# The triangular inverse of a gated delta rule, with the whole triangle as weights, masks applied on the way out of PSUM, and transposes for one of its products

## The reference

```python
def _gated_delta_rule(q, k, v, beta, g):
    ...
    decay = jnp.where(causal, jnp.exp(jnp.where(causal, diff, 0.0)), 0.0)
    kb = kc * bc[..., None]
    a_kk = jnp.einsum('nbhid,nbhjd->nbhij', kb, kc) * decay
    lhs = jnp.eye(CHUNK, dtype=jnp.float32) + jnp.tril(a_kk, -1)
    rhs = jnp.concatenate([vc * bc[..., None], kb * jnp.exp(G)[..., None]], axis=-1)
    sol = lax.linalg.triangular_solve(lhs, rhs, left_side=True, lower=True, unit_diagonal=True)
    u, w = sol[..., :dv], sol[..., dv:]
    ...
```

## Time and profile before

| | |
|---|---|
| median of 3 runs | 2108.77 us (2107.01 to 2109.0) |
| profiled execution, its own time | 2111.13 us |
| its span in the trace | 2109.1 us |
| TensorE busy, weight loads busy | 1738.8 us (82%), 1076.9 us (51%) |
| VectorE, ScalarE, GpSimd busy | 1359.3, 925.2, 905.4 us |
| granted TensorE clock, mean | 0.963 of full speed |
| gathers of the first mixture of experts | 174 to 815 us of the span |
| inverse stage (level 0 and the loop) | 987 to 1095 us |
| gathers of the second | 1441 to 2079 us |

### The profile page before, as it was taken

One profiled execution on the slowest core, in us unless ns is written; L12 is line 12 of the kernel. 1 busy time (PEld: TensorE's weight loads), 2 busy tenths in 40 slices (PEclk: granted clock), 3 DMA queues, 4 the chain that ended last, 5 costly groups with the idle time before them and its releaser, 6 DMA issues.

```text
span 2109.1 us, 22912 instructions
## 1 busy us (share of the span) xinstructions
PE 1738.8 (82%) x7686; PEld 1076.9 (51%) x7686; DVE 1359.3 (64%) x2924; ACT 925.2 (44%) x2363; POOL 905.4 (43%) x806
## 2 busy tenths in 40 slices
PE   8987988877787887897899977887988878778786
PEld 7985444322222222786898877785444323222222
DVE  3668667667766654698345377548677667767654
ACT  5555454444444444443234233455454444444443
POOL 3335333333333332566446288545333334333331
PEclk9998999999999999999999989998999999999999
DMA  6458999999999997342114412357999999999996
GB/s 224 135 165 315 420 420 420 421 421 421 422 422 421 421 421 311 109 132 80 41 31 117 133 61 80 119 181 301 420 421 422 421 421 421 422 421 421 422 421 283
DMA packets 102054, 637.16 MB, mean 302 GB/s; under 512 B 11264, under 2 KB 12544, under 8 KB 36272
## 3 DMA queue, kind: packets, MB, share of 16 engines
q0 software_dynamic: 75216, 543.27, 62.0%
q1 hardware_dynamic: 26720, 92.43, 14.0%
HBM read 634.61 MB, written 1.05 MB: 301 GB/s over the span
## 4 chain that ended last, share of the span: by engine, by line
PE 36%; DMA 35%; DVE 14%; ACT 7%; POOL 4%; issue 3%; SPq 0%; DVEq 0%; ACTq 0%; POOLq 0%
DMA arena<-in_uv,arena 27%; PE pb L587 15%; DMA spare<-in_uv,arena 8%; PE pb L336 4%; PE pb L338 4%; PE pb L337 4%; DVE arena L1559 3%; ACT arena L1007 3%; POOL parts L1995 2%; POOL arena L2053 1%; PE pb L409 1%; PE pb L700 1%; PE pb L714 1%; PE pb L709 1%; ACT arena L1002 1%
## 5 line engine op out<-in xcount | busy, mean ns | idle before, releaser
L587 PE MATMUL pb<-arena 128*128 128x512 f32 x1848 | 915.6, 625 | 228.0 <-ACT arena L1007 226.8
L1559 DVE SCALAR_TENSOR_TENSOR arena<-arena,pb 128x1024 f32<-128x1024 f32 x462 | 563.6, 1220 | 380.9 <-DMA arena<-in_uv,arena 380.5
L2017 POOL DMA_INDIRECT arena<-in_uv,arena x462 | 440.4, 953 | 723.7 <-PE pb L587 697.6
L587 PEld LDWEIGHTS pb<-arena 128*128 128x128 f32 x1848 | 324.6, 193 | 786.7 <-ACT arena L1007 520.0
L1995 POOL TENSOR_TENSOR parts<-ring,parts 128x512 fp32r<-128x512 f32 x228 | 337.0, 1493 | 332.8 <-ACT parts L850 311.6
L999 ACT ACTIVATE arena<-arena 128x1 f32<-128x1 f32 x512 | 103.3, 202 | 621.5 <-DVE arena L1559 562.2
L850 ACT ACTIVATE parts<-ring 128x512 fp32r<-128x512 f32 x328 | 201.9, 628 | 265.8 <-PE pb L338 260.7
L336 PE MATMUL pb<-xl,parts 128*128 128x256 f32 x704 | 223.5, 317 | 10.2 <-DVE xl L1253 6.0
L1007 ACT ACTIVATE arena<-cst,arena 128x128 f32<-128x128 f32 x512 | 205.5, 401 | 47.2 <-ACT arena L1002 0.4
L336 PE MATMUL pb<-parts,xh 128*128 128x256 f32 x608 | 183.0, 301 | 41.1 <-POOL parts L1995 30.5
L337 PE MATMUL pb<-xh,parts 128*128 128x256 f32 x704 | 202.8, 288 | 0.0
(11 more groups left out here) (289 smaller groups left out, 1872.8 us busy)
## 6 DMA issues: line engine op xcount, KB each, us to landing
ring<-in_w_in SPq DMA_DIRECT2D x108, 512.0 KB, 3.6
ring<-in_wq SPq DMA_DIRECT2D x32, 512.0 KB, 4.6
ring<-in_w_out SPq DMA_DIRECT2D x16, 512.0 KB, 3.6
arena<-in_uv,arena POOLq DMA_INDIRECT x462, 20.2
ring<-in_wa SPq DMA_DIRECT2D x8, 512.0 KB, 3.6
ring<-in_wb SPq DMA_DIRECT2D x8, 512.0 KB, 3.6
arena<-in_sk POOLq DMA_DIRECT2D x2, 1024.0 KB, 6.3
arena<-in_tail POOLq DMA_DIRECT2D x1, 1280.0 KB, 9.6
```

The source lines that it names most:

```text
L587: ins = pe.matmul(ys[hf][:, :], diags[:, k % 4, :], lands[k % LANDS][:, D + hf * 512:D + (hf + 1) * 512], start=k % (8 * K) == 0, stop=k % ...
L1559: ve.scalar_tensor_tensor(z, z, 1.0, xg[t], ALU.mult, ALU.mult, accum_out=hidden[:, k:k + 1]).then_inc(*up("v_dot", ("dot", e, k)))
L2017: gp.indirect_dma_start(lands[k % LANDS], None, rows_uv, bass.IndirectOffsetOnAxis(ap=eidx[:, k:k + 1], axis=0)).then_inc(*up(f"dma_rows{k ...
```

## The change

The weights of Y become the whole triangle `LT`, with ones set on its diagonal by a copy under a mask (VectorE, `copy_predicated`, once for each group at level 0). What Y keeps of the product is chosen on the way out of PSUM, by VectorE with one of 7 new constants `signs` (identity minus mask). The cutting of `ET` on GpSimd goes away, and `ET` with it. XT of the next level is then Y^T XT in its odd half of the columns alone (64 of 128 columns of each matrix), which VectorE copies over the old ones; X is got by transposing XT, and ScalarE copies its even half of the columns. The product dX and both subtractions are gone. TensorE's order in a step n is Y(n), XT(n-1), transposes for X(n-2). At level 0, XT is `LT` times `signs[0]`, and X its transpose, copied by ScalarE; this copy stands ahead of the Exp at L1107 in ScalarE's program. The 7 new constants make `cst` 896 columns wider.

```diff
+    for lev in range(NLEV):
+        mask = parts[4 + lev]
+        parts.append(np.eye(P) - (mask.T if lev else mask))
...
+        cst = sb("cst", 4 * P + 2 * NLEV * P)
         cols = sb("cols", 64 + 96 + 32)
...
+        signs = [cst[:, (4 + NLEV + k) * P:(5 + NLEV + k) * P] for k in range(NLEV)]
...
+            def inverse_turned(lev, g):
+                o = bank(("X", lev, g))
+                pq.wait_ge(*on(("XT", lev, g)))
+                for s in range(4):
+                    ins = pe.transpose(o[:, s * P:(s + 1) * P], XT[:, g, s, :], ident)
+                ins.then_inc(*full(("X", lev, g)))
...
-                o = bank(("E0", g))
-                pq.wait_ge(*on(("E", 0, g)))
-                for s in range(4):
-                    ins = pe.transpose(o[:, s * P:(s + 1) * P], ET[:, g, s, :], ident)
-                ins.then_inc(*full(("E0", g)))
+                inverse_turned(0, g)
...
             def inverse_y(lev, g):
                 o = bank(("Y", lev, g))
-                pq.wait_ge(*on(("E", lev, g)))
-                pq.wait_ge(*on(("X", lev - 1, g)))
+                pq.wait_ge(*on(("M", g)))
+                pq.wait_ge(*on(("taken", ("X", lev - 1, g))))
                 for s in range(4):
-                    ins = pe.matmul(o[:, s * P:(s + 1) * P], ET[:, g, s, :], X[:, g, s, :], start=True, stop=True)
+                    ins = pe.matmul(o[:, s * P:(s + 1) * P], LT[:, g, s, :], X[:, g, s, :], start=True, stop=True)
                 ins.then_inc(*full(("Y", lev, g)))
 
-            def inverse_x(lev, g):
+            def inverse_xt(lev, g):
+                o = bank(("XT", lev, g))
                 pq.wait_ge(*on(("taken", ("Y", lev, g))))
-                if lev < NLEV - 1:
-                    o = bank(("dX", lev, g))
-                    pq.wait_ge(*on(("XT", lev - 1, g)))
-                    for s in range(4):
-                        ins = pe.matmul(o[:, s * P:(s + 1) * P], XT[:, g, s, :], Y[:, g, s, :], start=True, stop=True)
-                    ins.then_inc(*full(("dX", lev, g)))
-                o = bank(("dXT", lev, g))
-                pq.wait_ge(*on(("XT", lev - 1, g)))
+                m = 2 ** lev
                 for s in range(4):
-                    ins = pe.matmul(o[:, s * P:(s + 1) * P], Y[:, g, s, :], XT[:, g, s, :], start=True, stop=True)
-                ins.then_inc(*full(("dXT", lev, g)))
-
-            before = None
-            for lev in range(1, NLEV):
-                for g in range(4):
-                    if (4 * lev + g) % 8 == 7:
-                        item()
-                    inverse_y(lev, g)
-                    if before:
-                        inverse_x(*before)
-                    before = (lev, g)
-            inverse_x(*before)
+                    z = XT[:, g, s, :].rearrange("p (n two m) -> p n two m", two=2, m=m)[:, :, 1, :]
+                    ins = pe.matmul(o[:, s * 64:(s + 1) * 64], Y[:, g, s, :], z, start=True, stop=True)
+                ins.then_inc(*full(("XT", lev, g)))
+
+            steps = [(lev, g) for lev in range(1, NLEV) for g in range(4)]
+            for n, (lev, g) in enumerate(steps):
+                if (4 * lev + g) % 8 == 7:
+                    item()
+                inverse_y(lev, g)
+                if n >= 1:
+                    inverse_xt(*steps[n - 1])
+                if n >= 2 and steps[n - 2][0] < NLEV - 1:
+                    inverse_turned(*steps[n - 2])
+            inverse_xt(*steps[-1])
...
                 copy(CT[:, 2 * c2:2 * c2 + 2, :], half(("back", c2)), ("back", c2))
+            for g in range(4):
+                copy(X[:, g], bank4(("X", 0, g)), ("X", 0, g))
             aq.wait_ge(*on("lb_less"))
             ac.activation(p2, p2, ACT.Exp).then_inc(*up("a_lb", "lb_exps"))
...
-            for lev in range(1, NLEV):
-                for g in range(4):
-                    if (4 * lev + g) % 8 == 7:
-                        item()
-                    key = ("Y", lev, g)
-                    if lev > 1:
-                        aq.wait_ge(*on(("XT", lev - 1, g)))
-                    copy(Y[:, g], bank4(key), key)
+            steps = [(lev, g) for lev in range(1, NLEV) for g in range(4)]
+            for n, (lev, g) in enumerate(steps):
+                if (4 * lev + g) % 8 == 7:
+                    item()
+                if n >= 2 and steps[n - 2][0] < NLEV - 1:
+                    lev, g = steps[n - 2]
+                    key = ("X", lev, g)
+                    copy(even(X[:, g], 2 ** lev), even(bank4(key), 2 ** lev), key)
             for g in range(4):
-                if g == 0:
-                    for z in range(4):
-                        aq.wait_ge(*on(("E", NLEV - 1, z)))
                 copy(U[:, g], bank4(("U", g)), ("U", g))
...
                 vq.wait_ge(*on(("taken", ("L", g))))
-                ve.tensor_tensor(ET[:, g], LT[:, g], bm(masks[0], 4), ALU.mult).then_inc(*up("v_inverse", ("E", 0, g)))
-                vq.wait_ge(*on(("E", 0, g)))
-                ve.tensor_tensor(XT[:, g], bm(ident, 4), ET[:, g], ALU.subtract).then_inc(*up("v_inverse", ("XT", 0, g)))
-                vq.wait_ge(*full(("E0", g)))
-                ve.tensor_tensor(X[:, g], bm(ident, 4), bank4(("E0", g)), ALU.subtract).then_inc(*taken(("E0", g)))
-                at[("X", 0, g)] = on(("taken", ("E0", g)))
+                ve.copy_predicated(LT[:, g], bm(ident.bitcast(U32), 4), bm(ones, 4)).then_inc(*up("v_inverse", ("M", g)))
+                vq.wait_ge(*on(("M", g)))
+                ve.tensor_tensor(XT[:, g], LT[:, g], bm(signs[0], 4), ALU.mult).then_inc(*up("v_inverse", ("XT", 0, g)))
...
-            def inverse_x(lev, g):
-                if lev < NLEV - 1:
-                    key = ("dX", lev, g)
-                    vq.wait_ge(*full(key))
-                    ve.tensor_tensor(X[:, g], X[:, g], bank4(key), ALU.subtract).then_inc(*taken(key))
-                    at[("X", lev, g)] = on(("taken", key))
-                key = ("dXT", lev, g)
+            def inverse_y(lev, g):
+                key = ("Y", lev, g)
                 vq.wait_ge(*full(key))
-                vq.wait_ge(*on(("XT", lev - 1, g)))
-                ve.tensor_tensor(XT[:, g], XT[:, g], bank4(key), ALU.subtract).then_inc(*taken(key))
+                ve.tensor_tensor(Y[:, g], bank4(key), bm(signs[lev], 4), ALU.mult).then_inc(*taken(key))
+
+            def inverse_xt(lev, g):
+                key, m = ("XT", lev, g), 2 ** lev
+                vq.wait_ge(*full(key))
+                ve.tensor_copy(odd(XT[:, g], m), pb[place[key]][:, 0:256].rearrange("p (s n m) -> p s n m", s=4, m=m)).then_inc(
+                    *taken(key))
                 at[("XT", lev, g)] = on(("taken", key))
 
-            before = None
-            for lev in range(1, NLEV):
-                for g in range(4):
-                    if (4 * lev + g) % 8 == 7:
-                        item()
-                    if before:
-                        inverse_x(*before)
-                    flush()
-                    before = (lev, g)
-            inverse_x(*before)
+            steps = [(lev, g) for lev in range(1, NLEV) for g in range(4)]
+            for n, (lev, g) in enumerate(steps):
+                if (4 * lev + g) % 8 == 7:
+                    item()
+                inverse_y(lev, g)
+                if n >= 1:
+                    inverse_xt(*steps[n - 1])
+                flush()
+            inverse_xt(*steps[-1])
...
-            for lev in range(1, NLEV):
-                for g in range(4):
-                    if (4 * lev + g) % 8 == 7:
-                        item()
-                    key = (("E0", g) if lev == 1 else ("Y", lev - 1, g))
-                    gq.wait_ge(*on(("full", key)))
-                    gq.wait_ge(*on(("XT", 0, g)))
-                    gp.tensor_tensor(ET[:, g], LT[:, g], bm(masks[lev], 4), ALU.mult).then_inc(*up("g_inverse", ("E", lev, g)))
+            for _ in range(3):
+                item()
```

More of the change, by code:

```diff
@@ L48 @@
     matmul = transpose = activation = tensor_copy = tensor_tensor = tensor_scalar = op
-    scalar_tensor_tensor = tensor_tensor_scan = tensor_reduce = reciprocal = memset = op
+    scalar_tensor_tensor = tensor_tensor_scan = tensor_reduce = reciprocal = memset = copy_predicated = op
     max = max_index = match_replace = dma_start = indirect_dma_start = then_inc = op
@@ L89, in build @@
         spare = sb("spare", 2 * D)
-        cst = sb("cst", 4 * P + NLEV * P)
+        cst = sb("cst", 4 * P + 2 * NLEV * P)
         cols = sb("cols", 64 + 96 + 32)
@@ L204, in build, with odd, even @@
         btv, kdv, eGv = v2(sv["beta"]), v2(sv["kd"]), v2(sv["eG"])
-        LT, X, XT, ET, Y = (region(o, 2048, g=4).rearrange("p g (s n) -> p g s n", s=4)
-                            for o in (6144, 8192, 24576, 26624, 28672))
+        LT, X, XT, Y = (region(o, 2048, g=4).rearrange("p g (s n) -> p g s n", s=4)
+                        for o in (6144, 8192, 24576, 28672))
+        def odd(ap, m):
```

(3 more changed lines are left out.)

## The result

The changed kernel takes 2094.63 us in the median of four runs (2093.54 to 2096.64); the kernel before, 2108.89 in four (2107.01 to 2109.93). The ratio is 0.9942, interval 0.9928 to 0.9956: 14.3 us less, faster by 0.6%, where 17.5 had been forecast (2091.3, range 2080 to 2100). The two profiled executions differ by 17.5 us (2111.13 and 2093.62), of which 14.0 lie in the stretch that the change touches. It took 111.5 us before and 97.5 after.

What follows compares the result with a forecast made beforehand. It took TensorE's fixed order of work in the inverse stage, 1003 to 1095 us, as the bound. Terms -9.1 - 10.0 - 3.6 + 2.9 + 2.2 + 0.1 = -17.5 us, from 2108.8, gave 2091.3; range 2080 to 2100.

Steps and rivals of the forecast that it cites:

- GpSimd leaves the loop: Inverse loop: TensorE's three waits for GpSimd's masks go, -10.0 us, and the slow clock behind them, -3.6 us.
- Nothing late next: After a weight product in the inverse loop: no new TensorE wait replaces the masks, by 0.2 us of slack.
- Transposes: Inverse loop, levels 1 to 5: 20 dX sets become groups of four transposes, 0.893 to 0.437 us each, -9.1 us.
- Half width: Inverse loop: 24 sets streaming 64 columns instead of 128 stay at 0.893 us, no gain; bounds nothing and 10.7 us.
- The row of 16 columns: Trace row of a 16-column product: instructions 0.12 us apart, the full sets' pace, taken as evidence that half width gains nothing.
- Level 0: Each group's ring (L, Q, mask, transposes, next L) lengthens by c + 0.04, c being copy_predicated's 0.69: +2.9 us over four.
- Scalar's queue: After level 0: table load and Exp behind the last X copy delay Vector and XT(1,0), +2.2 us once.
- The start: Kernel start: the constants' load grows by 448 KB; taken as costing nothing, with 1.1 us as upper end.
- rival 2: Longer waits bring the slower clock to level 0 and the four sets after: +8.4 us, 2099.7, chance 0.12.
- the narrow range: Whole kernel: the forecast case's own range, 2089 to 2096 us, from c, the start and a microsecond for run spread.

## Why the prediction was right or wrong

The range held the time, and the direction was right. By its steps:

- *GpSimd leaves the loop, -10.0 and -3.6.* Right: the waits and the slow clock behind the weight products are gone, and the run that moves only GpSimd's block shows that this term alone is 12 us of the stage, 13.8 with the wait of 1.6 that this run has in its place.
- *Nothing late next.* Right; VectorE even has `finish` done in 0.42 + 0.74 us, since GpSimd no longer runs beside it.
- *Transposes, -9.1.* Right: sets of 0.893 became 0.44, 9.0 us; 10.1 with products in their place.
- *Half width, 0.* Nearly: 0.84 for 0.893, 1.2 us more than reckoned, of bounds 0 and 10.7. The row of 16 columns was the right guide.
- *Level 0, +2.9.* Right: the ring of a group is 4.59 us (991.50 to 996.09 for L's evacuation), 0.76 more, c = 0.716: 3.0.
- *Scalar's queue, +2.2.* Right: 4.49 us from the last transposes' start to XT(1,0), 2.23 without the wait and at full clock, so 2.3. In this execution the Y sets ran at 1.2 GHz and TensorE stood still for only 0.9 of it. The table load starts 0.02 us behind the copy's end and is followed by the Exp at once; the drain that the Trainium skill counts (ScalarE: Activation LUTs, What ACT_TABLE_LOAD costs) shows nowhere, and the measurement decides.
- *The start, 0.* No run isolates it. In the profile after, the first user of the constants (L502) starts at 27.83 us, 28.64 before, and waits for nothing.

The step that failed is what the sum left out: "the clock stays at 1.00 through level 0" was taken from the kernel before and kept as the likeliest case, though the change itself lengthened the waits that it rests on. It was rival 2, with 8.4 us and a chance of 0.12; it came, from the fourth group on, in each of the five executions profiled with the waits of level 0 as they are in the change (two of the changed kernel, those with the Exp first, with full width and with products for the transposes), and in the changed kernel it costs 4.8 us. With it and the half width the sum is -17.5 + 4.8 - 1.2 = -13.9, for 14.0 in the stage. So apart from GpSimd's queue the change comes out even: -9.0 - 1.2 on TensorE against +3.0 + 2.2 + 4.8 at level 0 and behind it, which is why the run that moves GpSimd's blocks alone is as fast in the total. Forecast and the second rival were taken as alternatives where the second was a term: it should have stood in the sum, at the 1.7 to 1.9 us that a drop had cost behind single waits, or more. How long the clock stays down is not the same each time: until the first weight product in three of the five executions, until XT(1,0) in the other two.

Some of the hit is luck. The range of 2080 to 2100 had its upper end at the second rival, so it held the missing term by design; that the time also lies in the narrow range of 2089 to 2096, which left this term out, is chance. So is that the two profiled executions differ by just the forecast 17.5 us.

Of the 3.5 us between 14.0 in the stage and 17.5 in the two profiled executions' times, 1.7 lie ahead of the stage (its start at 985.7 for 987.4), in unchanged code, and 1.7 behind it. The changed kernel's own two profiled executions start the stage at 985.7 and 983.2, so such differences are the spread of executions; medians differ by 14.3. The prediction had called time gained outside 987 to 1100 us a sign of being wrong, which a single pair of executions can't show.

## What to carry to other kernels

Look first at what stands in front of the late instruction in its own engine's queue: here moving three blocks of GpSimd's program, each behind four small masks, was worth as much as rewriting the algorithm. When a change takes work off TensorE or lengthens its waits, cost the granted clock as a term of the sum; if waits can't be shortened, give TensorE other work in them. The cheapest gains were in the order of the work: a group ahead, and a product that fills the waits.

## What the runs showed of the hardware that was not expected

- Behind three waits of 2.2 us with TensorE about half busy (6.91 of 13.43 us) the granted clock fell to its lower level, at the fourth group's L product in all five executions with these waits, and 0.44 us of extra work in each wait kept it up through level 0. It also fell behind one wait of 2.1 us that followed a stretch as busy as 11.10 of 17.93 us, while one of 1.9 us left it up in another kernel.
- Transposes were enough as added work: with 4, 8 or 16 of them in each of these waits, TensorE kept the full clock through level 0.
- A product of f32 with 64 moving columns takes 0.84 us for eight instructions, one with 128 takes 0.89.
- VectorE beside GpSimd: a copy under a mask took 1.57 us for 0.72, an operation on 16 elements a partition 1.20 for 0.17, while evacuations with one operand in PSUM kept their 0.69. The Trainium skill (VectorE: DVE Perf Modes, Two Vector instructions with no wait between them) says that the second SBUF input of a VectorE instruction is read through an interface shared with GpSimd; both slow operations have two SBUF inputs, and the trace agrees. It is not all: `finish`, which has one tensor as input beside its scalars, takes 1.62 us for two instructions beside GpSimd's masks and 0.74 in the kernel after, where GpSimd stands still.
